# Expert stage of a routed block: gate and up columns cut in strips of 128, down rows cut in blocks of 128

## The reference

```
hid = silu(xblk @ w_gate[e]) * (xblk @ w_up[e])      # w_gate, w_up: 1024 x 512
y   = hid @ w_down[e]                                # w_down:       512 x 1024
```

## Time and profile before

| | |
|---|---|
| median of 3 runs | 909.4 us (907.77 to 909.72) |
| profiled execution, its own time | 911.11 us |
| its span | 909.3 us |
| PE busy | 775.5 us (85%), 5393 records |
| VectorE, ScalarE busy | 373.5 us (41%), 168.4 us (19%) |
| moved by DMA | 284.38 MB, mean 313 GB/s |
| mean granted TensorE clock | 0.949 of full |

### The profile page before, as it was taken

The page is one execution under the profiler, slowest core; times in us unless marked ns, Lnnn a source line. Parts: engine busy times, 40 slices in busy tenths (PEclk is TensorE's granted clock), DMA queues, the critical chain, the costliest instruction groups (busy, mean ns, idle before and its releaser), DMA issues.

```text
span 909.3 us, 13058 instructions
## 1 busy us (share of the span) xinstructions
PE 775.5 (85%) x5393; PEld 465.6 (51%) x5393; DVE 373.5 (41%) x885; ACT 168.4 (19%) x473; POOL 40.5 (4%) x36
## 2 busy tenths in 40 slices
PE   7999899999998999999999987858766686677655
PEld 3544664456476644456578573535534444344332
DVE  2478668557854676766441212111111111121113
ACT  3222630223356301041120100000010100001001
POOL 1110000012400000001000000000000000000000
PEclk9999999999999999999999997889899889899888
DMA  9984506765002749987679999999999999999994
GB/s 343 394 291 155 186 1 241 269 231 186 1 1 82 277 130 352 392 338 321 232 269 396 406 425 430 430 430 427 426 427 429 430 428 429 427 428 429 427 428 162
DMA packets 54555, 284.38 MB, mean 313 GB/s; under 512 B 2800, under 2 KB 7280, under 8 KB 41968
## 3 DMA queue, kind: packets, MB, share of 16 engines
q1 hardware_dynamic: 54512, 283.81, 78.0%
HBM read 282.75 MB, written 1.05 MB: 312 GB/s over the span
## 4 chain that ended last, share of the span: by engine, by line
PE 55%; DMA 34%; DVE 5%; issue 2%; ACT 2%; POOL 1%; SPq 1%; DVEq 0%; POOLq 0%
DMA ring<-in_up_w 30%; PE banks L2002 15%; PE banks L1850 9%; PE banks L2413 8%; PE banks L2248 4%; DMA ring<-in_down_w 3%; PE banks L1954 3%; PE banks L2461 2%; PE banks L1882 2%; PE banks L2398 2%; DMA ring<-in_ada_w 1%; PE banks L1929 1%; POOL rs L590 1%; PE banks L1980 1%; PE banks L2492 1%
## 5 line engine op out<-in xcount | busy, mean ns | idle before, releaser
L2413 PE MATMUL banks<-ring,QT 128*32 128x256 f32 x1696 | 143.0, 445 | 56.7 <-DMA ring<-in_up_w 56.7
L2002 PE MATMUL banks<-ring,hT 128*128 128x512 f32 (+4 forms) x384 | 157.9, 566 | 2.4 <-DMA ring<-in_ab_w 2.1
L2413 PEld LDWEIGHTS banks<-ring,QT 128*32 128x32 f32 x1696 | 71.9, 123 | 105.7 <-DMA ring<-in_up_w 44.1
L2002 PEld LDWEIGHTS banks<-ring,hT 128*128 128x128 f32 x384 | 72.4, 193 | 75.5 <-issue 68.6
L1746 DVE TENSOR_TENSOR QT<-banks,MOD 32x256 f32<-32x256 f32 x128 | 53.8, 421 | 138.5 <-PE banks L2461 137.2
L1737 DVE TENSOR_TENSOR QT<-QT,banks 64x256 f32<-64x256 f32 x32 | 13.5, 423 | 191.4 <-ACT QT L943 191.4
L1850 PE MATMUL banks<-ring,hT 128*128 128x512 f32 x192 | 83.9, 594 | 1.9 <-ACT hT L628 1.8
L2461 PE MATMUL banks<-ring,QT 128*32 128x256 f32 x992 | 66.0, 408 | 14.6 <-ACT QT L950 12.4
L590 POOL TENSOR_TENSOR rs<-st,mhalf 128x1 f32<-128x1 f32 (+7 forms) x27 | 33.3, 1237 | 863.3 <-DVE st L1783 451.7
L943 ACT ACTIVATE QT<-banks 64x256 f32<-64x256 f32 x32 | 12.0, 375 | 294.4 <-PE banks L2413 294.4
L1185 DVE SCALAR_TENSOR_TENSOR extra<-ring,cs,extra 128x512 f32<-128x512 f32 x84 | 63.1, 752 | 2.9
(11 more groups left out here) (361 smaller groups left out, 767.6 us busy)
## 6 DMA issues: line engine op xcount, KB each, us to landing
ring<-in_down_w SPq DMA_DIRECT2D x30, 2048.0 KB, 21.8
ring<-in_up_w SPq DMA_DIRECT2D x30, 2048.0 KB, 23.6
ring<-in_gate_w SPq DMA_DIRECT2D x23, 2048.0 KB, 20.4
ring<-in_ada_w SPq DMA_DIRECT2D x12, 2048.0 KB, 15.4
probs<-in_gate_w SPq DMA_DIRECT2D x8, 2048.0 KB, 29.2
ring<-in_ab_w SPq DMA_DIRECT2D x4, 2048.0 KB, 19.4
ring<-in_cd_w SPq DMA_DIRECT2D x4, 2048.0 KB, 13.5
ring<-in_in_w SPq DMA_DIRECT2D x4, 2048.0 KB, 14.5
```

The lines of the kernel that those rows point to most:

```text
L2002: ins = pe.matmul(bank[b][:, 0:n], hT[:, k, t * P:(t + 1) * P], w[:, k, :], start=(k == 0), stop=(k == KD - 1))
L2413: return pe.matmul(bank[1][CAP * j:CAP * j + CAP, 0:256], XG[:, k, CAP * s:CAP * s + CAP], wk[:, :, 2 * (j % 2):2 * (j % 2) + 2], start=(k ...
```

## The change

- Gate and up are done one behind the other for every expert, each on four strips of 128 neighbouring hidden columns, so that `bank[1]` holds gate in columns 0 to 127 and up in 128 to 255, on all 128 partitions. The number of matmuls of `gate_up` doubles (32 to 64) and each streams 128 columns instead of 256.
- A gate slot comes free when gate is done (`g_gate_n`), an up slot when up is done (`g_gu`). PE waits for up only after gate's matmuls, and for the second half of the gathered tokens (expert 0) after 4 of gate's 8 k.
- Silu and product work on 128 partitions x 128. `turn_hidden` is one `pe.transpose` of 128 x 128.
- The rows of `w_down` are loaded by `"e (c p) n -> p (e c) n"`: partition p gets rows p, 128 + p, 256 + p, 384 + p, four pieces of 4 KB that lie 512 KB apart. This holds for all down weights, those loaded ahead and the last ones too.
- `idx` and `g_gate` share a semaphore through `stages("_n", ...)`.

```
-        SIG = qt_flat[64:128, 2048:2304]
-        HID = qt_flat[0:64, 2304:2560]
+        SIG = qt_flat[:, 2048:2176]
+        HID = qt_flat[:, 2176:2304]
...
-                    lambda e: down_w[bass.ds(e, 1), :, :].rearrange("e (p c) n -> p (e c) n", c=FC)]
+                    lambda e: down_w[bass.ds(e, 1), :, :].rearrange("e (c p) n -> p (e c) n", c=FC)]
...
-                sp.wait_ge(*upto("g_down" if j % 3 == 2 else "g_gu", freed_by + 1))
+                sp.wait_ge(*upto(("g_gate_n", "g_gu", "g_down")[j % 3], freed_by + 1))
...
-                act.activation(SIG, bank[1][0:64, 0:256], ACT.Silu).then_inc(sem("g_sig"), 1)
+                act.activation(SIG, bank[1][:, 0:P], ACT.Silu).then_inc(sem("g_sig"), 1)
...
-                v.tensor_tensor(HID, SIG, bank[1][64:128, 0:256], ALU.mult).then_inc(sem("g_hid"), 1)
+                v.tensor_tensor(HID, SIG, bank[1][:, P:2 * P], ALU.mult).then_inc(sem("g_hid"), 1)
...
-                def strip(k, j):
-                    wk = (wg, wu)[j // 2](k).rearrange("p (f c) -> p f c", c=FC)
-                    return pe.matmul(bank[1][CAP * j:CAP * j + CAP, 0:256], XG[:, k, CAP * s:CAP * s + CAP],
-                                     wk[:, :, 2 * (j % 2):2 * (j % 2) + 2], start=(k == 0), stop=(k == KD - 1))
...
+                for w, j in ((wg, 0), (wu, 1)):
+                    gathered_landed(pe, q, s, j)
                     for k in range(KD):
...
+                        if first_quad(q) and s == 0 and (j, k) == (0, 4):
                             pe.wait_ge(*upto("g_xv", 1))
...
+                        for n in range(4):
+                            ins = pe.matmul(bank[1][CAP * n:CAP * n + CAP, P * j:P * j + P], XG[:, k, CAP * s:CAP * s + CAP],
+                                            w(k)[:, P * n:P * n + P], start=(k == 0), stop=(k == KD - 1))
+                    ins.then_inc(sem(("g_gate_n", "g_gu")[j]), 1)
...
-                for j in range(2):
-                    ins = pe.matmul(hidden_psum(q)[:, 64 * j:64 * j + 64], HID[:, j:256:2], ident[0:64, 0:64],
-                                    start=True, stop=True)
-                ins.then_inc(sem("g_ht"), 1)
+                pe.transpose(hidden_psum(q)[:, 0:P], HID, ident).then_inc(sem("g_ht"), 1)
...
-                    a = 64 * (c % 2) + CAP * (c // 2)
...
-                        ins = pe.matmul(bank[2][CAP * n:CAP * n + CAP, 0:256], HG[:, a:a + CAP],
+                        ins = pe.matmul(bank[2][CAP * n:CAP * n + CAP, 0:256], HG[:, CAP * c:CAP * c + CAP],
                                         wd(c)[:, 256 * n:256 * n + 256], start=(c == 0), stop=(c == FC - 1))
```

More of the change, by code:

```diff
@@ L116, in build @@
         stages("_mm", [("abin", 12), ("about", 4), ("cdin", 12), ("cdout", 4), ("win", 8), ("wout", 4)])
+        stages("_n", [("idx", 2), ("g_gate", NE)])
         stages("_Pa", [("abin", 6), ("cdin", 6), ("win", 4)])
@@ L738, in _ @@
             for t in range(NT):
-                act.wait_ge(*upto("idx", t + 1))
+                act.wait_ge(*upto("idx_n", t + 1))
                 for odd in range(2):
@@ L2053, in _ @@
                                     QT[r, 10 + h // 2, t * P:(t + 1) * P], QT[r, 12, 0:K], start=True, stop=True)
-                ins.then_inc(sem("idx"), 1)
+                ins.then_inc(sem("idx_n"), 1)
             for t in range(NT):
@@ L2358, in expert @@
                         for k in range(KD):
-                            ins = pe.matmul(bank[c][:, a:a + SEQ], w(k)[:, c:512:FC], hT[:, k, :],
+                            ins = pe.matmul(bank[c][:, a:a + SEQ], w(k)[:, P * c:P * c + P], hT[:, k, :],
                                             start=(k == 0), stop=(k == KD - 1))
@@ L2409, in gate_up @@
                 wg, wu = gathered_weight(q, s, 0), gathered_weight(q, s, 1)
-                def strip(k, j):
-                    wk = (wg, wu)[j // 2](k).rearrange("p (f c) -> p f c", c=FC)
-                    return pe.matmul(bank[1][CAP * j:CAP * j + CAP, 0:256], XG[:, k, CAP * s:CAP * s + CAP],
-                                     wk[:, :, 2 * (j % 2):2 * (j % 2) + 2], start=(k == 0), stop=(k == KD - 1))
-                gathered_landed(pe, q, s, 0)
-                if last:
-                    for k in range(KD):
-                        for j in range(2):
[L2420 to L2428, removed]
+                for w, j in ((wg, 0), (wu, 1)):
+                    gathered_landed(pe, q, s, j)
+                    for k in range(KD):
+                        if first_quad(q) and s == 0 and (j, k) == (0, 4):
                             pe.wait_ge(*upto("g_xv", 1))
-                        for j in range(4):
-                            ins = strip(k, j)
-                ins.then_inc(sem("g_gu"), 1)
+                        for n in range(4):
+                            ins = pe.matmul(bank[1][CAP * n:CAP * n + CAP, P * j:P * j + P], XG[:, k, CAP * s:CAP * s + CAP],
+                                            w(k)[:, P * n:P * n + P], start=(k == 0), stop=(k == KD - 1))
+                    ins.then_inc(sem(("g_gate_n", "g_gu")[j]), 1)
             def turn_hidden(q, s):
```

## The result

The change makes the kernel slower: 917.99 us (915.93 to 920.01, 4 runs) against 908.87 us for the kernel before on the same chip, a ratio of 1.0101 with the interval 1.0074 to 1.0128. That is +9.1 us. The forecast was 912.6 us, +3.2, with a range up to 916.6. The direction is right and the size is three times too small. The profiled execution after took 915.93 us, span 914.1; it is the fastest of the four.

A forecast was written before the change was run, and what follows sets the result against it. Transfers at 428 GB/s were taken to bound the kernel from about 545 us. Dearer down packets +5.1 us, less 1.1 and 0.8 at the start, gave +3.2 us on 909.4, so 912.6 us, range 907.3 to 916.6.

The forecast's parts named there:

- What bounds the kernel: From about 545 us to down 30's landing, transfers at 428 GB/s set the end, 4.90 us a load; faster TensorE gains nothing.
- Part 1: Down loads: 4 KB packets instead of 16 KB cost 0.18 us a load over 28 loads, +5.1 us (bounds 0 and 11.8).
- Part 2: Start of the expert stage: expert 1's down ends 1.1 us sooner, and 0.8 us is regained at down 6.
- the bullet on `gate_up` in Part 2: Start of the stage: twice the matmuls at half length keep the rate, 3.63 us; shorter last latency gives -0.1 us.
- Part 3: Middle of the expert stage: slots come free sooner, but about five loads are queued already and cover a later PE: 0.
- the -1.9 us of the start: Start of the expert stage: the total saving forecast there, 1.1 us at expert 1's down and 0.8 us at down 6.
- Part 4: Tail behind down 30's landing: down 30's and 31's matmuls unchanged, 0; PE idle about 3 us before could add +2 to +3.
- the rival: Cold tail or dearer packets: clock falls while PE idles before down 30; forecast plus 2 to 3 us, 914.6 to 917; chance 0.13.
- the case of 0.13: Tail: cold clock or dearer packets, forecast plus 2 to 3 us, 914.6 to 917; chance 0.13.
- 13.6 us from the last landing to the end: Tail: a sign to look for in the profile after, 13.6 us from the last landing to the span's end.

The follow-up runs named there:

- e0: The changed kernel run once more, unedited, for its spread and a second trace: 918.41 us, ratio 1.0105.
- e2: The kernel before with only the new down rows (4 KB pieces 512 KB apart) and the matching choice of columns: 913.62 us, ratio 1.0057.
- e8: The kernel before with the gate and up matmuls of experts 0 to 3 alone cut into two of 128 columns: 909.53 us, ratio 1.0005.
- e9: The kernel before with the gate and up matmuls of experts 4 to 27 alone cut in two: 909.47 us, ratio 1.001.
- e6: The changed kernel with down rows in two 8 KB pieces a partition and strips taking every second column of a half: 914.0 us, ratio 1.0055.
- e10: The changed kernel with expert 31's gate and up done two strips at a time, same number of instructions: 917.04 us, ratio 1.0096.
- e5: The changed kernel, but a gate slot is refilled only when up is done too, as before: 918.7 us, ratio 1.0104.
- e3: The kernel before with every gate and up matmul of experts 0 to 30 cut into two of 128 columns: 912.59 us, ratio 1.0036.
- e4: The changed kernel with expert 31's gate and up matmuls each done twice: 918.44 us, ratio 1.0108.
- e7: The changed kernel with 8 KB down pieces and expert 31's gate and up matmuls done twice: 913.97 us, ratio 1.0057.
- e12: The kernel before with the gate and up matmuls of experts 28 to 30 alone cut in two: 910.95 us, ratio 1.0023.
- e1: The changed kernel with down rows back in 16 KB pieces and strips taking every fourth column: 925.6 us, ratio 1.0185.

## Why the prediction was right in direction and wrong in size

**What bounds the kernel: right.** Transfers set the end before and after; 421 GB/s from 545 to 890 us were measured where 423 were forecast.

**Part 1, the packets: right mechanism, somewhat low.** The price can be read between two landings in the steady stretch, those of the up loads of experts 9 and 29, which are 20 down loads apart. The first are the landings at 543.73 + 23.32 = 567.05 us in before and at 542.61 + 23.01 = 565.62 in after; the second, before and then after:

```profile
835.75 24.94 DMA ring<-in_up_w
```
```profile
836.02 27.84 DMA ring<-in_up_w
```

That is 860.69 - 567.05 = 293.6 us and 863.86 - 565.62 = 298.2 us. e0 and e2 have 298.1, e8 and e9, whose packets are those of before, 293.7. So a down load of 4 KB packets costs 0.22 to 0.23 us more; the forecast had 0.18. 28 loads make 6.2 to 6.4 us, where the forecast had 5.1 and e2, timed, 5.2 (3.2 to 7.2). The price sets in above 4 KB already: with 8 KB pieces (e6) 16 down loads take 236.2 us against 234.9, 0.08 us a load. The Trainium skill's rule ("DMA: Bandwidth & Descriptors", Specifications), by which pieces of 512 B and more go at line rate, does not hold here: 421 against 428 GB/s with a third of the loads in 4 KB pieces.

**Part 2, the start: the terms are right, the gain is not seen.** Silu takes 278 ns, the product 288, the turn 296, and 128 records of `gate_up` 3.49 to 3.67 us, all as forecast. The issue of down 3 ends 484.03 - 466.53 = 17.5 us after the stage's first matmul, before 486.58 - 467.62 = 19.0: 1.5 us sooner, forecast 1.1. Down 6 is 48.9 against 50.8 us, 1.9 us sooner, forecast 2.7: here the waits for instructions (3.8 us until then) have eaten a part. Yet the up load lands 99.1 us after the stage's start in after, 101.6 in e0 and 99.8 in e10, in before 99.4, in e2 99.1. Six down loads with dearer packets (0.225 us each) and the gain of 1.9 should have made 98.9. e2, which has the same packets and the old order of gate and up, issues down 6 even sooner, 512.28 - 465.82 = 46.5 us after the start, and its up load lands no earlier. Profiles of the same code differ by over 2 us here, so what the start returned, between 0 and the 1.9 us, stays open; no run shows the gain that the forecast subtracted. That the early gate release is worth nothing by itself (e5) was forecast.

**The step that failed** is the bullet on `gate_up` in Part 2, "So I take no change in rate", together with Part 3's "The same backlog covers a PE that is up to several us later per expert". The rate is indeed unchanged, but the number of instructions was costed at nothing. Twice the instructions bring waits in which TensorE has its operands and stands: 6.7 us in 5 in after. e3 times them at +3.3 us (1.0 to 5.6) in the kernel before, with nothing else changed, and there the backlog covers them in the middle, as Part 3 says, and not in the last quad (+2.1 of the 3.5 us). That they are waits for TensorE's own instructions is read from four things: no operand or semaphore ends them, the instruction queue carries 33 packets for 27, they appear and vanish with the number of instructions (e3, e4, e7, e8), and each of 28 in nine traces ends 2.2 to 2.7 us after a packet of that queue. Two more terms of the sum failed beside it: the -1.9 us of the start, which no landing shows, and the 0 of Part 4.

**Part 4, the tail: "None of these changes: 0" was wrong in the profile, where the rival came true.** PE is idle for 3.15 us ahead of down 30 and the matmuls take 3.62 us. The windows of the kernel after, over the idle time and over down 30 in two parts:

```profile
890.70:893.80 3.10, 0.00 (x0) 0.00 (x0) 0.29 (x1) 0.28 (x1) 0.00 (x0) 1.00 1.03 411
893.90:896.00 2.10, 2.10 (x24) 1.05 (x28) 0.00 (x0) 0.00 (x0) 0.00 (x0) 0.51 0.94 373
896.00:897.40 1.40, 1.40 (x16) 0.38 (x8) 0.00 (x0) 0.00 (x0) 0.00 (x0) 0.52 0.59 240
```

The granted clock (the third value from the end) is still 1.00 in the idle time and 0.51 in the matmuls behind it, 1.2 in place of 2.4 GHz. In e10, with 2.24 us of idle time, it stays at 1.00. The forecast had put this aside as the case of 0.13. It was priced at 2 to 3 us; from landing to end after takes 20.3 us, against 19.2 before and 17.6 in e2, e8 and e9, so the profiles give 1.1 to 2.7. (The 19.2 of before has a slow stretch of its own: the last outputs are spread in 3.61 us where e2, e8 and e9 need 1.97.) e10, which takes a part of the idle time away, gives back 1.4 in its profile and 0 to 0.8 as timed. The forecast's 13.6 us from the last landing to the end does not follow from its rows: the second half of down 31 starts at 895.00, 14.3 us ahead of the end.

**The sum as it was measured.** Packets 5.2 (e2) and instructions 3.3 (e3) make 8.5 us; the tail adds up to 2.7 by the profiles and up to 0.8 by the times, the start takes off between 0 and 1.9. Measured are 9.1 and, for e0, 9.2 to 9.5. So the sum closes, but each term is known to about 2 us, and it is not shown that e3's cost carries over whole. In the kernel before two thirds of it lie in the last quad, where TensorE has no time to spare. In the changed kernel TensorE stands idle for 3.15 us ahead of down 30, and neither of its two profiles has such a wait in `gate_up` behind 545 us. Only the waits at the start are sure to be there, and e8 and e9, which have them, cost 1.4 us together, neither clear of nothing. The landings give another sum that closes as well: packets 6.3, which leaves 2.8 us for the waits at the start and the cold tail together. e6 leaves the same: 5.0 less 28 x 0.08 = 2.2 is 2.8. How the part beyond the packets divides between instructions, clock and the missing gain stays open. No version of the change that ran was as fast as the kernel before.

## What to carry to other kernels

When transfers bound a kernel, count the packets of each load first: a layout that cuts a partition's piece from 16 KB to 4 KB cost 4.6% of that load here (0.22 to 0.23 of 4.9 us), one to 8 KB under 2%. Count instructions as a resource as well; splitting a matmul at an unchanged rate was not free here (+3.3 us in e3), least of all in the last quad, where TensorE worked right up to the last transfers (+2.1 us in e12). And an engine made faster ahead of a transfer that sets the end gets only idle time, and may pay for it with its clock, as in after (3.62 us for 32 records in place of 1.93).

## What the runs showed of the hardware that was not expected

A moving operand with a step of four float32 columns halves the rate of four column strips: 7.48 us for the 128 matmuls of e1, against 3.49 to 3.88 with neighbouring columns or every second one, and 3.63 for 64 of double length with pairs out of fours. The Trainium skill ("SBUF — State Buffer", "Door 1: The DMA port swizzle") tells of 16-byte lines that want at least two hits each for full bandwidth, and the cases agree: one hit a line in e1, two with pairs or every second column, four with neighbouring ones.

TensorE can stand for up to 3.2 us (e10, at 497.29 us; 2.6 in after) with every operand ready. Such waits are at nearly the same places in e0 as in after, and they end 2.2 to 2.7 us after a packet of the instruction queue, so an edit meant to fill idle time with more instructions (e4, e7) can bring in a new wait.
